# Gate/up pairs of a SwiGLU layer: three 2x2 blocks of seven products instead of two, with two weight sums moved off the vector engine

## The reference

```python
def _swiglu(x, w_gate, w_up, w_down):
    return (jax.nn.silu(x @ w_gate) * (x @ w_up)) @ w_down

x = _layer_norm(DEEPNORM_ALPHA * x + _dsa_mixer(x, *mix_p), ln1_g, ln1_b)
x = _layer_norm(DEEPNORM_ALPHA * x + _swiglu(x, w_gate, w_up, w_down), ln2_g, ln2_b)
```

## Time and profile before

| what | value |
|---|---|
| runs shown | 931.02, 931.09, 931.32 us; median 931.09 |
| profiled execution, its own time | 931.67 us |
| its span, first to last instruction | 929.9 us |
| PE / DVE / ACT / POOL busy | 923.4 / 773.7 / 513.4 / 95.9 us |
| DMA | 188.06 MB, 202 GB/s on the mean |

### The profile page before, as it was taken

One profiled execution on the slowest core, in us unless ns is written; L12 is line 12 of the kernel. 1 busy time (PEld: TensorE's weight loads), 2 busy tenths in 40 slices (PEclk: granted clock), 3 DMA queues, 4 the chain that ended last, 5 costly groups with the idle time before them and its releaser, 6 DMA issues.

```text
span 929.9 us, 11643 instructions
## 1 busy us (share of the span) xinstructions
PE 923.4 (99%) x4406; PEld 774.5 (83%) x4406; DVE 773.7 (83%) x1049; ACT 513.4 (55%) x704; POOL 95.9 (10%) x84
## 2 busy tenths in 40 slices
PE   9999999999999999999999999999999999999997
PEld 8999988888878888888888888888888888888885
DVE  6778566578779898989999998988969997999777
ACT  5686765354464646555565646455545565456550
POOL 0205530000311020202011020000000000000000
PEclk9999999999999999999999999999999999999999
DMA  9744324584808375665648375756657656355632
GB/s 362 315 166 145 129 91 167 195 328 167 318 5 290 111 256 162 223 218 185 228 135 274 112 270 148 242 198 200 219 210 300 226 225 233 130 222 231 230 132 91
DMA packets 36759, 188.06 MB, mean 202 GB/s; under 512 B 4064, under 2 KB 4576, under 8 KB 22880
## 3 DMA queue, kind: packets, MB, share of 16 engines
q1 hardware_dynamic: 36672, 187.32, 56.4%
q0 software_dynamic: 32, 0.00, 0.0%
HBM read 183.11 MB, written 4.19 MB: 201 GB/s over the span
## 4 chain that ended last, share of the span: by engine, by line
PE 99%; DVE 0%; ACT 0%; DVEq 0%; issue 0%; ACTq 0%
PE acc L1983 26%; PE acc L2005 21%; PE acc L1758 9%; PE tp L1983 9%; PE acc L1966 6%; PE acc L1696 5%; PE tp L1966 4%; PE tp L2005 4%; PE acc L1617 4%; PE acc L1895 2%; PE tp L1935 2%; PE acc L1730 1%; PE tp L1809 1%; PE tp L1744 1%; PE tp L1822 1%; PE tp L1606 0%
## 5 line engine op out<-in xcount | busy, mean ns | idle before, releaser
L1983 PE MATMUL acc<-w_hi,act_t 128*128 128x512 f32 x720 | 227.3, 389 | 0.0
L972 ACT ACTIVATE w_hi<-raw 128x1024 fp32r<-128x1024 f32 x120 | 125.7, 1057 | 111.4 <-PE acc L1983 57.2
L1021 ACT ACTIVATE w_hi<-raw 128x512 fp32r<-128x512 f32 (+1 forms) x154 | 114.9, 782 | 100.3 <-PE acc L2005 88.0
L2005 PE MATMUL acc<-w_hi,hid_t 128*128 128x512 f32 x504 | 161.0, 389 | 0.0
L1424 DVE TENSOR_TENSOR w_lo<-raw,w_hi 128x512 fp32r<-128x512 f32 (+1 forms) x154 | 131.8, 881 | 33.2 <-ACT w_hi L1021 33.0
L1983 PEld LDWEIGHTS acc<-w_hi,act_t 128*128 128x128 f32 x720 | 135.1, 188 | 28.1
L1377 DVE TENSOR_TENSOR w_lo<-raw,w_hi 128x1024 fp32r<-128x1024 f32 x120 | 147.2, 1244 | 7.7 <-ACT w_hi L972 6.9
L1983 PE MATMUL acc<-w_lo,act_t 128*128 128x512 f32 x360 | 140.0, 389 | 0.0
L2005 PEld LDWEIGHTS acc<-w_hi,hid_t 128*128 128x128 f32 x504 | 94.6, 188 | 19.6
L2005 PE MATMUL acc<-w_lo,hid_t 128*128 128x512 f32 x252 | 98.0, 389 | 0.0
L1374 DVE TENSOR_TENSOR w_lo<-raw,w_hi 128x1024 fp32r<-128x1024 f32 x63 | 82.7, 1313 | 18.2 <-ACT w_hi L967 17.8
(11 more groups left out here) (262 smaller groups left out, 1582.2 us busy)
## 6 DMA issues: line engine op xcount, KB each, us to landing
raw<-in_w_pairs SPq DMA_DIRECT2D x120, 512.0 KB, 4.5
raw<-in_w_down SPq DMA_DIRECT2D x44, 1024.0 KB, 6.0
raw<-in_w_pairs SPq DMA_DIRECT2D x18, 1024.0 KB, 7.6
raw<-in_w_out SPq DMA_DIRECT2D x16, 1024.0 KB, 4.9
raw<-in_w_gu SPq DMA_DIRECT2D x8, 1024.0 KB, 10.7
raw<-in_x_w SPq DMA_DIRECT2D x14, 552.0 KB, 7.1
raw<-in_w_uq SPq DMA_DIRECT2D x4, 1024.0 KB, 6.1
raw<-in_w_ukv SPq DMA_DIRECT2D x4, 1024.0 KB, 4.8
```

The source lines that it names most:

```text
L972: act.activation(w_hi[:, v % RING, :], plain_raw(m), ACT.Copy).then_inc(hi_done, 1)
L1021: act.activation(unit_parts(u)[0], block_of(b, block, width), ACT.Copy).then_inc(down_hi_done, 1)
L1983: last = pe.matmul(out[:, t, :], act_t[:, k0 + m, x, t * P:(t + 1) * P], part[:, v % RING, m * GC:(m + 1) * GC], start=False, stop=(end an ...
L2005: last = pe.matmul(bank, lhs(x), part[:, cols * GC:(cols + 1) * GC], start=(first == u and (cols, x) == (0, 0) and part is hi_), stop=(end ...
```

## The change

- PAIR_K becomes 6: three 2x2 blocks. 10 k stay plain, 5 steps for each tile. The blocks are handled as "two" (two of them, 128x1024) and "third" (one, 128x512), so each product is two steps, of 6 and 3 matmuls: 7 x 9 + 2 x 5 x 12 = 183 matmuls in a pair.
- The ring is given out in blocks of 512 columns (8 of them, `ring_places`): a full step takes two neighbours, a "third" one, and one is skipped where a full one doesn't fit at the end. A step's high part waits for the last step that held its blocks (`BEFORE`). Silu, the seeds and `gate_up` are placed before the first step that takes the freed place (`FREED`).
- The order is new: P1, P2, P5, P6 are interleaved with the five "second" steps of the pair before, then come P7, P3, "first 0", P4, "first 1" to "first 4". The "second" steps of tile 1 from its fourth half on belong to this list as well (p = 0).
- T1 = B11 + B12 is made by a DMA that GpSimd issues and that adds B12 from memory onto B11 once B11's low part is made. T3 = B12 + B22 is a GpSimd sum per block, placed behind the low parts of "first 3", "first 4" and "second 0", where DVE does its transposes. T2 and T4 stay with DVE.
- The factor sums of hid and their low part go from GpSimd to DVE, behind "second 1" and behind P6 "third".
- GpSimd's sums of `act_t` at the beginning cover three blocks instead of two, and the block sums of pair 1 come before `s_gate`'s low part on its queue.
- SP issues the next pair's three block loads together, behind plain block 4 of ten.

```diff
 PAIRS = TILES // 2
-PAIR_K = 4
+BLOCKS = 3
+PAIR_K = 2 * BLOCKS
...
     for p in range(1, PAIRS):
-        ends = [(p - 1, "second", n) for n in range(PLAIN - 3, PLAIN)] if p > 1 else [None] * 3
-        for product, end in zip((P1, P5, P6), ends):
-            steps += [(p, "product", product), end]
-        steps += [(p, "product", n) for n in (P7, P2, P3)] + [(p, "first", 0), (p, "product", P4)]
-        steps += [(p, "first", n) for n in range(1, PLAIN)] + [(p, "second", n) for n in range(PLAIN - 3)]
-    steps += [(PAIRS - 1, "second", n) for n in range(PLAIN - 3, PLAIN)]
+        steps += [(p, "two", P1), (p - 1, "second", 0), (p, "third", P1), (p - 1, "second", 1)]
+        for product, end in zip((P2, P5, P6), range(2, PLAIN)):
+            steps += [(p, "two", product), (p, "third", product), (p - 1, "second", end)]
+        steps += [(p, part, product) for product in (P7, P3) for part in ("two", "third")]
+        steps += [(p, "first", 0), (p, "two", P4), (p, "third", P4)]
+        steps += [(p, "first", n) for n in range(1, PLAIN)]
+    steps += [(PAIRS - 1, "second", n) for n in range(PLAIN)]
...
+HID_AT = 3
+TURN_STEPS = ("first", 2), ("first", 3), ("first", 4), ("second", 0)
...
+    widths = [1 if kind == "third" else 2 for _, kind, _ in FFN_STEPS]
+    widths += [unit[3] for unit in DOWN_UNITS[:len(DOWN_UNITS) - LAST_LATE]]
+    at, places, before = 2 * (V_PAIRS % RING), {}, {}
+    held = {2 * (v % RING) + x: v for v in range(V_PAIRS - RING, V_PAIRS) for x in range(2)}
+    for v, width in enumerate(widths, V_PAIRS):
+        if at + width > RING_BLOCKS:
+            at = 0
+        places[v], before[v] = at, max(held[x] for x in range(at, at + width))
+        held.update((x, v) for x in range(at, at + width))
+        at = (at + width) % RING_BLOCKS
...
+FREED = {v: min(w for w in BEFORE if BEFORE[w] >= v) for v in range(V_PAIRS, V_DOWN)}
...
 (SP)
-                    if n in (PLAIN, PLAIN + 1):
-                        if p < PAIRS - 1:
-                            load_quad(p + 1, n - PLAIN)
-                        else:
-                            load_down(n - PLAIN)
+                    if n in (PLAIN, PLAIN + 1) and p == PAIRS - 1:
+                        load_down(n - PLAIN)
+                    if n == PLAIN_SLOTS and p < PAIRS - 1:
+                        for q in range(BLOCKS):
+                            load_quad(p + 1, q)
...
 (ACT)
+                        if v == FREED[V_OF[p, "third", n]]:
                             if n == P1:
                                 act.wait_ge(ffn_hid, 2 * p - 1)
+                            act.wait_ge(*used_step(V_OF[p, "third", n]))
                             act.activation(dst, second[:, 1, :], ACT.Copy, scale=sign).then_inc(seeded, 1)
...
 (DVE)
+            def sum_2(p, kind):
+                part = two if kind == "two" else third
+                dve.tensor_tensor(part(p, B11), part(p, B11), part(p, B22), ALU.add).then_inc(t2_done, 1)
+            def sum_4(p, kind):
+                part = two if kind == "two" else third
+                dve.wait_ge(t2_done, 2 * (p - 1) + (1 if kind == "two" else 2))
+                dve.tensor_tensor(part(p, B21), part(p, B11), part(p, B21), ALU.add).then_inc(t4_done, 1)
+            def factor_sums(q):
+                if q > 0:
+                    dve.wait_ge(s_lo, q)
+                dve.wait_ge(ffn_turned, q + 1)
+                dve.tensor_tensor(s_sum[:, S3, :], a11, a21, ALU.subtract).then_inc(s_step, 1)
+                dve.wait_ge(s_step, 4 * q + 1)
+                dve.tensor_tensor(a21, a21, a22, ALU.subtract).then_inc(s_step, 1)
+                dve.wait_ge(s_step, 4 * q + 2)
+                dve.tensor_tensor(s_sum[:, S2, :], a21, a11, ALU.subtract).then_inc(s_step, 1)
+                dve.wait_ge(s_step, 4 * q + 3)
+                dve.tensor_tensor(s_sum[:, S4, :], a12, s_sum[:, S2, :], ALU.add).then_inc(s_step, 1)
+            def factor_low(q):
+                dve.wait_ge(s_hi, q + 1)
+                dve.tensor_tensor(s_t[:, q, 1, :, :], s_sum[:], s_t[:, q, 0, :, :], ALU.subtract).then_inc(s_lo, 1)
...
             for p, kind, n in FFN_STEPS:
                 before_lo(V_OF[p, kind, n])
                 lo_step(p, kind, n)
+                if n == P5 and kind in ("two", "third"):
+                    sum_2(p, kind)
+                if n == P6 and kind in ("two", "third"):
+                    sum_4(p, kind)
+                if (kind, n) == ("first", 1):
                     add_y(p)
+                if (kind, n) == ("second", 1) and 0 < p <= len(DOWN_QUADS):
+                    factor_sums(p - 1)
+                if (kind, n) == ("third", P6) and 0 <= p - 2 < len(DOWN_QUADS):
+                    factor_low(p - 2)
+                if (kind, n) in TURN_STEPS and p > 0:
+                    turn_hid(p - 1, TURN_STEPS.index((kind, n)))
...
 (POOL)
+            def load_t1(p, kind):
+                blocks = w_pairs[p - 1][:, 0:BLOCKS * RAW_ELEMS].rearrange("p (q e) -> p q e", q=BLOCKS)
+                b12 = blocks[:, :, B12 * GC:(B12 + 1) * GC]
+                pool.wait_ge(lo_done, V_OF[p, kind, P1] + 1)
+                if kind == "two":
+                    pool.dma_start(two(p, B11), b12[:, 0:2, :], accum_op=ALU.add).then_inc(t1_two, 16)
+                else:
+                    pool.dma_start(third(p, B11), b12[:, 2, :], accum_op=ALU.add).then_inc(t1_third, 16)
+            def t3_sum(p, q):
+                if p > 1:
+                    pool.wait_ge(lo_done, V_OF[(p - 1,) + TURN_STEPS[1 + q]] + 1)
+                pool.wait_ge(quad_full[q], 16 * p)
+                b12, b22 = ((two(p, B12)[:, q, :], two(p, B22)[:, q, :]) if q < 2 else
+                            (third(p, B12), third(p, B22)))
+                pool.tensor_tensor(b12, b12, b22, ALU.add).then_inc(t3_done, 1)
+            def block_sums(p):
+                t3_sum(p, 0)
+                t3_sum(p, 1)
+                load_t1(p, "two")
+                t3_sum(p, 2)
+                load_t1(p, "third")
+            block_sums(1)
             pool.wait_ge(g_hi, 1)
+            pool.tensor_tensor(s_gate[:, 1, :, :, :], g_sum[:, :, 0:2, :], s_gate[:, 0, :, :, :], ALU.subtract)
+            pool.tensor_tensor(s_third[:, 1, :, :], g_sum[:, :, 2, :], s_third[:, 0, :, :], ALU.subtract)\
+                .then_inc(g_lo, 1)
+            for p in range(2, PAIRS):
+                block_sums(p)
...
 (PE)
+                    if n in (P2, P7, P4):
+                        pe.wait_ge(seeded, 3 * p - 2 + (P2, P7, P4).index(n))
```

More of the change, by code:

```diff
@@ L667, in _ @@
             load_tile(1)
+            load_quad(1, 2)
             sp.wait_ge(x1_done, TOK * CHUNKS)
@@ new lines, in _, with sum_wait @@
+            SOURCE = {P1: B11, P5: B11, P6: B11, P7: B12, P2: B21, P3: B22, P4: B21}
+            def sum_wait(p, kind, n):
+                q = 2 * (p - 1) + (kind == "third")
+                if n == P1:
+                    for b in (0, 1) if kind == "two" else (2,):
+                        act.wait_ge(quad_full[b], 16 * p)
+                elif n == P5:
+                    act.wait_ge(t1_two if kind == "two" else t1_third, 16 * p)
+                elif n == P6:
+                    act.wait_ge(t2_done, q + 1)
+                elif n == P7:
+                    act.wait_ge(t3_done, BLOCKS * (p - 1) + (2 if kind == "two" else 3))
+                elif n == P4:
+                    act.wait_ge(t4_done, q + 1)
@@ L999, in _ @@
                 hi_step(p, kind, n)
-                if (kind, n) == ("second", PLAIN - 4):
+                if (p, kind, n) == (0, "second", 1):
+                    gate_sums_hi()
+                if (kind, n) == ("second", HID_AT) and p > 0:
                     hid_hi(p - 1)
-                if (kind, n) == ("product", P5) and 2 <= p < len(DOWN_QUADS) + 2:
+                if (kind, n) == ("third", P5) and 2 <= p < len(DOWN_QUADS) + 2:
                     q = p - 2
@@ L1372, in lo_step @@
                 dve.wait_ge(hi_done, v + 1)
-                if kind == "product":
-                    dve.tensor_tensor(by_quad(w_lo[:, v % RING, :]), quad(p, LOW_OF[n]), by_quad(w_hi[:, v % RING, :]),
+                if kind == "two":
+                    cols = ring(v, 2)
+                    dve.tensor_tensor(by_quad(ring_lo[:, cols]), two(p, LOW_OF[n]), by_quad(ring_hi[:, cols]),
+                                      ALU.subtract).then_inc(lo_done, 1)
+                elif kind == "third":
+                    cols = ring(v, 1)
+                    dve.tensor_tensor(ring_lo[:, cols], third(p, LOW_OF[n]), ring_hi[:, cols],
@@ new lines, in _ @@
+            a11, a12, a21, a22 = (turned[:, 0, c, t * P:(t + 1) * P] for t in range(TOK) for c in range(2))
+            def factor_sums(q):
[9 more added lines that the diff above has]
+                dve.tensor_tensor(s_sum[:, S4, :], a12, s_sum[:, S2, :], ALU.add).then_inc(s_step, 1)
@@ L1988, in _ @@
             first_tile()
-            tile_1()
+            for h in range(HALVES_1):
```

(9 more changed lines are left out.)

269 lines of the change are left out of this document (121 added, 148 removed).

## The result

| | before | changed |
|---|---|---|
| median of the timed runs | 931.21 us (931.02 to 931.71) | 942.46 us (941.71 to 944.41) |
| ratio, 95% interval | 1 | 1.0123 (1.0106 to 1.0141) |
| profiled execution, its span | 931.67, 929.9 us | 943.05, 941.2 us |
| matmuls | 4406 | 4376 |

A forecast was written before the change was run, and what follows sets the result against it. The prediction took TensorE's matmuls as the bound until another engine makes it wait. Its terms, -6.8 - 1.0 + 7.1 + 0.9 + 1.0 + 2.4 = +3.6 us, gave 934.7 us, range 925.5 to 941.

The forecast's parts named there:

- What is removed: On PE, 30 fewer matmuls over ten pairs, -6.8 us, and pair 1's wait for ScalarE's seed gone, -1.0 us.
- The tight place: From P5 to the plain step after P6, VectorE's 9.70 us of work makes PE wait in pairs 2 to 10: +7.1 us.
- VectorE keeps up: Rival, chance 0.19: VectorE's work fits beside PE's matmuls, so the tight-place and seed waits vanish: 925.3 us.
- half of it: Rival, chance 0.18: tight place costs only 0.5 us in seven pairs, with no seed wait: 929.8 us.
- the beginning: Before tile 1, GpSimd's longer act_t sum locks VectorE out, +1.0 us; its later work to pair 1's s4 adds 2.4.
- The third seed: Before "first 0" in pairs 2, 5 and 8, ScalarE's seed comes 0.3 us late, three times: +0.9 us.
- Pair 1, +2.4: From tile 1's start to pair 1's s4, GpSimd's 10.8 us of work delays VectorE and so PE: +2.4 us.
- DMA: Three block loads take 7.9 us, the plain load behind has about 1 us to spare, adding transfers are in time: no cost.
- The adding transfer: GpSimd's DMA between P1's low part and P5's high part, taken as 4.5 us against 8.9 and 6.3 allowed: costs nothing.
- rival of the late transfer: Rival, chance 0.10: the adding transfer takes up to 7.6 us and P5 "third" waits, 1.3 us in ten pairs: 947.7 us.
- Transposes locked out: Rival, chance 0.05: GpSimd's block sums also block VectorE's transposes, some 3.2 us in nine pairs: 963.5 us.
- the free one: Reading that GpSimd's sums leave VectorE's one-input transposes undisturbed; under it the forecast sum stands.

The follow-up runs named there:

- number 9: Number 7's kernel with both adding transfers cut to 8 elements per block and partition (output not the reference's): 926.08 us.
- number 3: The changed kernel with the factors' low part made behind P3 "third" instead of behind P6 "third": 936.69 us.
- 4: The changed kernel with the low and high parts of hid made behind s4, the fifth "second" step, for all pairs but the last: 934.83 us.
- Number 7: The kernel of versions 6 with ScalarE's copy of y placed behind the third seed instead of before P4: 929.88 us.
- number 8: Number 7's kernel with GpSimd waiting for the low part of tile 1's first half before the sums of act_t: 933.29 us.
- Number 1: The changed kernel with the next pair's third block load issued behind plain block 5 instead of before it: 938.24 us.
- number 10: The changed kernel with only both adding transfers cut to 8 elements per block and partition (output not the reference's): 942.49 us.
- versions 6: The changed kernel with the four edits of Number 1, 2, number 3 and 4 together: 931.17 us.
- 2: The changed kernel with GpSimd waiting for the low part of pair 1's P2 "two" before making s_gate's low part: 936.24 us.

## Why the prediction was wrong

- **What is removed** (-6.8 and -1.0): right. The changed kernel without its gaps and without the slow clock would have a span of 941.2 - 18.8 = 922.4; number 9, whose gaps cost 2.4, has 924.2, which makes 921.8.
- **The tight place, +7.1**: right in mechanism, place and size (0.87 per pair, taken as 0.9; 9.70 us of VectorE's work as computed), and shown by numbers 3 and 4. *VectorE keeps up* is refuted. The average that spoke for it (40.6 of 41.5) is a poor witness: number 9 has VectorE busy 41.36 us of a 43 us stretch (355 to 398), with PE never idle. The rival *half of it* named 2.4 for the beginning and added 2.0; with 2.4 it gives 930.2 and not 929.8.
- **The third seed, +0.9, and the beginning, +1.0**: right, 0.8 and 0.9. Number 7 shows the first, number 8 the second.
- **Pair 1, +2.4**: the mechanism was right and the size off; 4.8 measured. The account spread GpSimd's 10.8 us over the whole stretch up to s4. But the rows from 247.05 to 265.75 sum to 18.3 us, since beside VectorE they took longer than the prices used (1.9 for a 128x384 sum in place of 0.9, about 2.0 for a block sum in place of 1.2), and 5.4 us of what VectorE lost fell on one low part, at P2, with little of PE's work ahead of it. And the lower clock behind the idle time (1.6 us) wasn't in the sum: in the kernel before PE never idles so long in this stage (0.98 at the earlier trace rows), and no row of before showed it.
- **DMA, "about 1 to spare" and "costs nothing"**: this is the step that failed, 5.2 us. Two things were missed. The plain load behind the block loads was taken to land 10.3 to 11.3 us after the first of them was issued; it landed 13.3 after (330.42 to 343.74). The block loads themselves landed at 337.43, 339.88 and 342.37, the last 12.0 us after the first issue, and the first alone took 7.0. The 7.9 of the forecast took the rate of a stretch in which the engines were already full, without a start-up of their own and without the plain loads that run beside them. And the need was reckoned by s0's own step alone. The Silu waits for the transposes, which wait for s0's low part, and s1's high part stands behind the Silu, which ties s1 to the load of s0 as well. That wait is a line of the kernel before (`act.wait_ge(ffn_turned, i // 2)`), and there, with another order of loads and steps, it showed no idle PE. Number 1 shows that the load's place is the cause; that the Silu's wait passes it on is read from the timeline, and wasn't tried alone.
- **The adding transfer** was assumed to take 4.5 us; it took 7.7 and 5.5. In the changed kernel P5's high parts waited for it in only three pairs, 5.0 us in all (2.9 in pair 1, 1.9 in pair 4, 0.3 in pair 7), and number 10 shows that PE lost nothing by it that can be told from the spread: 942.49 against 942.46. The one trace of it is the 1.18 before s4 in pair 4, which is 1.02 in number 10. The 8.9 us allowed for "two" were about right: from the low part's end (344.14) to P5's high part (353.99) are 9.9, with PE's own gap of 0.8 in between. By the fit that I named from the Trainium skill (DMA: Bandwidth & Descriptors, Anatomy of one DMA), an estimate of 3.2 and 2.6 us, it would have been far from any gate; the measured times are more than twice that. The rival of the late transfer (0.10) did not come true here, but it did in versions 6 and 7, before s3, once the other waits were removed; there the transfers also took longer themselves (9.5 and 8.5, 9.3 and 8.3). With number 1's edit alone they took 8.0 and 5.6, so the moved block load by itself doesn't explain that, and the cause is open.
- **Transposes locked out** (0.05): refuted, 1.78 to 1.80 us in all 27 groups of four that lie beside a GpSimd sum. So of the two readings of the Trainium skill (GPSIMD Engine Reference, Key points) this trace bears out the free one: VectorE's two-input work and GpSimd's contend (6.66 us for 1.22), a one-input transpose doesn't.

The range took in the bounds of terms that I had, and had no room for a step taken as zero. Either miss alone, the 5.2 before s1 or the 2.4 more in pair 1, would have left the time within 941; it took both. A margin of "about 1 us" ten times over is a rival with a price (ten times what it is missed by), not a step that costs nothing.

**What remains of the change.** Fully ordered it is worth 0.13%; 3.8 us more lie in the adding transfers, which no full version got back. The single edits 1, 2 and 4 gained 4.2, 6.2 and 7.6, together 18.0 (number 3 gained 5.8, but acts on the same gap as 4); all four at once gained 11.3. Part of the difference is those transfers; the rest, I read, without a run that shows it, is that a pair which waits in one place gives the loads time and waits less in the next.

## What to carry to other kernels

A producer engine at 96% of the bound engine's time can be hidden (41.36 of 43 in number 9), but only by the order: write down, for each slot, what it does between the slot's release and the next need, and sum up single pitches; that sum was right to 0.01 us here. Do the same for each load whose place in its queue moves, and follow it through every wait behind it, to the steps that don't read its data but stand behind an instruction that waits for those that do. After each wait that is removed, look for what it covered.

## What the runs showed of the hardware

- GpSimd's two-input instructions in close order kept a two-input instruction of VectorE waiting through three of them (6.66 us instead of 1.22); with two of them and another start, VectorE got in between (3.41 and 2.31). What decides it is open.
- GpSimd's sums were stretched as well: 1.87 to 1.99 us for 128x384 and about 2.0 for 128x512 beside VectorE's low parts in pair 1, and 1.28 for 128x512 beside a transpose.
- After 3.3 us without matmuls and 1.3 us with them again, the granted clock fell to the lower level for 3.4 us (268.3 to 271.7; 1.6 us lost) in the profiled executions of the changed kernel and of numbers 1 and 4, but not in those of 3 and 10, whose gap there is the same (3.33). In number 8, behind a gap of 3.67, it was low for 6.8 us (266.5 to 273.4). The way from P2 to P5 took 6.48 us with it and 4.88 without (starts in the changed kernel, then in number 10):

```profile
273.47 0.39 PE L2058 MATMUL tp<-w_hi,s_gate 128*128 128x512 f32 x1
```

```profile
267.24 0.47 PE L2058 MATMUL acc<-w_hi,act_t 128*128 128x512 f32 x1 [2.94 <-DVE w_lo L1409]
...
272.12 0.39 PE L2058 MATMUL tp<-w_hi,s_gate 128*128 128x512 f32 x1
```

- A transfer cut to 8 KB still took 5.7 us to land from GpSimd's queue in number 9, beside plain loads (DMA share 0.50 to 0.67), and 3.1 in pair 1 (share 0.20); the 4 KB ones took 2.4 and 2.7.
- A 128x128 sum on VectorE in a chain of dependent ones has a pitch of 0.32 us, 0.36 having been assumed.
